# A two-block transformer's opening: small loads on the ACT queue, fewer warming products, two modulation rows moved past a phase border

## The reference, cut to what matters

```python
c_act = jax.nn.silu(c)                                    # c: (1, 1024)
mod = (c_act @ ada_w[layer] + ada_b[layer])[:, None, :]   # the modulation vectors
sh_a, sc_a, gt_a, sh_m, sc_m, gt_m = jnp.split(mod, 6, axis=-1)
h = rms_norm(x, attn_norm[layer]) * (1 + sc_a) + sh_a     # modulate
q, k, v = jnp.split(h @ w_in, 3, axis=-1)                 # diff_attention, head by head
```

## Time and profile before

| | us |
|---|---|
| median of three runs | 2323.18 |
| the three runs | 2322.82, 2323.18, 2329.31 |
| the profiled execution | 2325.73 |
| its span in the profile | 2324.0 |
| PE busy, share of the span | 2227.1 (96%) |
| DVE busy | 1222.9 (53%) |
| ACT busy | 518.9 (22%) |

### The profile page before, as it was taken

How to read it: one execution, slowest core, us unless ns; L and a number is a source line. 1 busy time by engine, 2 the same in 40 slices (tenths; PEclk the granted TensorE clock), 3 DMA queues, 4 the chain that set the end, 5 groups by cost and what they waited for, 6 DMA issues and landing times. The chain is left out here.

```text
span 2324.0 us, 26617 instructions
## 1 busy us (share of the span) xinstructions
PE 2227.1 (96%) x9804; PEld 1495.2 (64%) x9804; DVE 1222.9 (53%) x2805; ACT 518.9 (22%) x1187; POOL 41.4 (2%) x49
## 2 busy tenths in 40 slices
PE   8999999999999999999999999999999899999976
PEld 4444688888887555558888888854578444444332
DVE  5455666667766266676655767668565311111104
ACT  4333223230003244442323100112232000000001
POOL 0000000000000000000000000000000010000100
PEclk9999999999999999999999999999998999999998
DMA  9455123534433211114534435311032799999996
GB/s 361 170 199 199 73 73 150 213 145 181 181 145 118 73 55 55 56 45 153 209 146 184 178 149 204 155 72 73 1 145 96 290 427 426 426 427 424 426 427 249
DMA packets 46419, 452.07 MB, mean 195 GB/s; under 512 B 7560, under 2 KB 8840, under 8 KB 21456
## 3 DMA queue, kind: packets, MB, share of 16 engines
q1 hardware_dynamic: 39440, 436.04, 47.0%
q0 software_dynamic: 6240, 12.17, 1.4%
q10 hardware_dynamic: 608, 2.14, 0.2%
HBM read 443.36 MB, written 17.87 MB: 198 GB/s over the span
## 5 line engine op out<-in xcount | busy, mean ns | idle before, releaser
L1404 PE MATMUL ps<-big,ring 128*128 128x256 f32 x768 | 186.0, 379 | 0.6 <-PE ps L1319 0.6
L3282 PE MATMUL ps<-big 128*64 128x512 f32 (+1 forms) x416 | 171.6, 606 | 7.8 <-ACT big L3337 5.0
L1319 PE MATMUL ps<-hT,ring 128*128 128x256 f32 x768 | 178.2, 380 | 0.0
L1319 PEld LDWEIGHTS ps<-hT,ring 128*128 128x128 f32 x768 | 144.8, 190 | 23.1 <-ACT hT L452 4.0
L1404 PEld LDWEIGHTS ps<-big,ring 128*128 128x128 f32 x768 | 145.6, 190 | 21.0 <-issue 1.4
L584 PE MATMUL ps<-hT,ring 128*128 128x512 f32 x336 | 151.7, 600 | 0.0
L3282 PE MATMUL ps<-ring,big 128*64 128x512 f32 (+1 forms) x336 | 134.0, 594 | 11.4 <-ACT big L3337 6.6
L2333 PE MATMUL ps<-hT,ring 128*128 128x512 f32 x320 | 140.7, 594 | 2.7 <-DVE big L2715 1.7
L1216 DVE SCALAR_TENSOR_TENSOR ring<-ring,tmp 128x1024 f32<-128x1024 f32 x112 | 136.3, 1218 | 0.0
L1404 PE MATMUL ps<-oT 128*128 128x256 f32 x512 | 120.8, 379 | 2.1 <-DVE oT L1583 2.1
L1319 PE MATMUL ps<-oT 128*128 128x256 f32 x512 | 115.8, 379 | 0.0
(11 more groups left out here) (550 smaller groups left out, 3893.7 us busy)
## 6 DMA issues: line engine op xcount, KB each, us to landing
ring<-in_stream SPq DMA_DIRECT2D x98, 2048.0 KB, 8.8
big<-in_up SPq DMA_DIRECT2D x18, 2048.0 KB, 22.7
ring<-in_down SPq DMA_DIRECT2D x17, 2048.0 KB, 22.0
ring<-in_gate SPq DMA_DIRECT2D x15, 2048.0 KB, 22.9
big<-in_gate SPq DMA_DIRECT2D x10, 2048.0 KB, 20.4
big<-in_down SPq DMA_DIRECT2D x8, 2048.0 KB, 21.9
ring<-in_up SPq DMA_DIRECT2D x6, 2048.0 KB, 18.8
oT<-in_up SPq DMA_DIRECT2D x5, 2048.0 KB, 28.2
```

The source lines that it names most:

```text
L1319: ins = pe.matmul(place(i, name), a[:, k, :], b[:, k, :], start=(k == 0), stop=(k == 3))
L1404: ins = pe.matmul(m.ps[:, bank[name], q * H:(q + 1) * H], a[:, q * P:(q + 1) * P], b, start=(first and q == 0), stop=(final and q == 1))
L3282: ins = pe.matmul(out[a:z, :], left[:, k * P + a:k * P + z], bufs[j][:, k * width + c * 512:k * width + (c + 1) * 512], start=(k == 0), st ...
```

## The change

It moves three loads from SP's queue to ACT's, ahead of ACT's first wait; it takes four of the six warming products between the sums and the spreading of the norm out; and it moves rows 2 and 3 of chunk 0, with the release of its slot, from `phase_start` to `phase_diff`, behind the first tile of `unit_rows`. The waits on `first_done` are counted anew.

```diff
@@ phase_start, sync
-                sp.dma_start(m.vec[:, 0:VEC_FIRST], m.d_vec[:, 0:VEC_FIRST]).then_inc(small, 16)
-                sp.dma_start(con(m, "ident"), m.d_con[:, 0:P]).then_inc(consts, 16)
-                sp.dma_start(buckets(m.con), buckets(m.d_con)).then_inc(consts, 16)
                 sp.dma_start(m.xT[:], m.d_x.rearrange("(k p) t -> p k t", p=P)).then_inc(xin, 16)
@@ phase_start, scalar
+                act.dma_start(m.vec[:, 0:VEC_FIRST], m.d_vec[:, 0:VEC_FIRST]).then_inc(small, 16)
+                act.dma_start(con(m, "ident"), m.d_con[:, 0:P]).then_inc(consts, 16)
+                act.dma_start(buckets(m.con), buckets(m.d_con)).then_inc(consts, 16)
                 act.wait_ge(small, 16)
@@ phase_start, vector
                 dve.reciprocal(m.st[:, 0:NT], m.st[:, 0:NT]).then_inc(inverse, 1)
-                for j in range(2, 4):
-                    first_modulation(m, dve, 0, j, crow).then_inc(mod_done, 1)
-                dve.wait_ge(mod_done, 4)
-                dve.sem_inc(m.free[0], 1)
+                dve.wait_ge(mod_done, 2)
@@ phase_start, tensor
-                keep_busy(m, pe, 0, 6)
+                keep_busy(m, pe, 0, 2)
@@ phase_diff, scalar
-                    if k >= 2:
-                        act.wait_ge(first_done, 2 * k - 2)
+                    if k:
+                        act.wait_ge(first_done, 2 * k)
@@ phase_diff, vector, first_columns
-                    dve.wait_ge(m.full[n % RING], 16 * (n // RING + 1))
-                    for j in range(4):
-                        first_modulation(m, dve, c, j, crow).then_inc(first_done, 1)
-                    dve.wait_ge(first_done, 4 * c)
+                    if c:
+                        dve.wait_ge(m.full[n % RING], 16 * (n // RING + 1))
+                    for j in range(4 if c else 2):
+                        first_modulation(m, dve, c, j if c else 2 + j, crow).then_inc(first_done, 1)
+                    dve.wait_ge(first_done, 4 * c + 2)
                     dve.sem_inc(m.free[n % RING], 1)
@@ phase_diff, vector
-                for c, tiles in ((1, range(0, 3)), (2, range(3, 6)), (3, range(6, KT))):
+                for c, tiles in ((0, range(0, 1)), (1, range(1, 3)), (2, range(3, 6)), (3, range(6, KT))):
                     for k in tiles:
                         unit_rows(k)
                     first_columns(c)
```

## The result

The changed kernel took 2336.85 us in the median of six runs (2333.64 to 2339.97), the kernel before 2327.89 beside it: ratio 1.0046, interval 1.0032 to 1.006. A second comparison of the same two, twelve runs against 35, gave 1.0033 (1.0022 to 1.0043). That is 8 to 11 us slower, at or over the 0.3% (7 us) that can be told; 2325.9 had been forecast, within 2321.4 to 2329.2. One run of a later kernel, the moved rows alone, took 4002.93 us at a granted clock of 0.628 and is left out of its ratio.

What follows compares the result with a forecast made beforehand. DVE's and PE's lines were both taken to bind the opening, with PE busy behind it. Rows and warming +1.2 plus moved loads +1.5 gave +2.7 us on 2323.18: 2325.9, range 2321.4 to 2329.2.

Steps and rivals of the forecast that it cites:

- Moved loads: Opening, three small loads on ACT's queue: x's packets beside them delay the tables by 1.5 us, bounds -0.2 and +3.3.
- The vector starts level with x: Opening loads: reason for taking 1.5 us, nearer the lower end, instead of the 40 KB store's 3.3.
- rival C: Opening: x goes ahead of the tables; tables +3.3 to +4.8 us, sum +4.5 to +6.0, up to 2329.2; chance 0.21.
- The lower bound: Moved loads: -0.2 us, by three issues at the 0.35 of ACT's row instead of about 0.42.
- E: Opening: ACT loads its table first and issues the loads from 2.03, 1.3 us more, 2327.2; chance 0.03.
- Warming products and moved rows: Before the first head's projection: border 1.08 us earlier, DVE's line to tile 6 1.36 later, PE gets it 1.2 later.
- B: Opening: tables land as before or 0.2 sooner, PE's line decides, warming products give 1.7 us; 2321.4; chance 0.12.
- Handed on as it is: Behind the opening: PE is busy without pause, so any shift of the opening's end passes on unchanged.
- One sign of being wrong: Behind 60 us: the prediction is wrong if stretches there differ in length.
- D: First head's projection: TensorE's clock stays at half throughout, +19 us, 2342; chance 0.02.

Runs made afterwards that it cites:

- the delays of 2, 3, 5 and 9 fills: The kernel before with the opening's loads held back by 2, 3, 5 or 9 one-tile fills on DVE: ratios 1.0013, 1.0024, 1.0014, 1.0033.

## Why the prediction was wrong

**Moved loads: the step that failed.** "One x packet between each two: 18 x 0.084 = +1.5", taken between -0.2 and +3.3. It measured **+3.9**, beyond the upper bound I gave the term. "The vector starts level with x" was true of the vector, which came 1.1 late. The tables are issued 0.47 and 0.95 behind it, and by then x had the engines: that is rival C's place and mechanism, given 0.21, and its price for the tables (+3.3 to +4.8) held the measured one. That the head's end came to C's far +6.0 is luck: C had 4.8 for the tables there, and nothing for the sums below. The 5.7 us of the small transfer on ACT's queue was the nearest row, and I set it aside as a store behind a long backlog; x alone is backlog enough. The lower bound fell too, as ACT's issues took 0.43 to 0.45 each and not 0.35; and so did E, as ACT issued at 0.75.

The Trainium skill, page "DMA: Bandwidth & Descriptors", section "Issuing engines are not separate DMA queues", says that such transfers interleave on the same 16 engines; the two kernels with x and the small loads apart and swapped agree (2.3 and 6.6 us). Its "Queues, rings and completion order" has an engine drain a packet of typically 9 to 17 descriptors from one queue before it turns; the trace's 153 packets of x in 4 to 5 us (2 KB each, 9.6 for each engine), with none of ACT's queue, are in line with that. The order within one engine was not seen.

**Warming products and moved rows: right, in mechanism and size.** Without the moved loads the border came 1.18 earlier (1.08 forecast), tile 6 came 1.36 later (1.36), and the head's end 0.95 and 1.16 later (1.2). DVE's line, with 0.15 of slack, did take back more than the warming gave. B, by which PE's line decides, is refuted.

**The sums: not foreseen.** In the changed kernel's first profile 3.89 at the bias product becomes 3.58 at ACT's copy and 4.99 at ACT's root. In between lie the sums over partitions, 6.99 us instead of 5.58. Their rows, of the changed kernel, of before and of the loads alone:

```profile
16.89 6.99 PE L344 MATMUL ps<-ones,hT 128*128 128x1 f32 x32 [2.05 <-DVE hT L318]
```

```profile
13.31 5.58 PE L347 MATMUL ps<-ones,hT 128*128 128x1 f32 x32 [1.36 <-DVE hT L318]
```

```profile
17.17 4.96 PE L347 MATMUL ps<-ones,hT 128*128 128x1 f32 x32 [1.24 <-DVE hT L318]
```

One row of the changed kernel, 17 to 24 us, and two of before, 13.31 to 15 and 15 to 22 us, show the clock:

```profile
17.00:24.00 7.00, 7.00 (x33) 7.00 (x34) 4.37 (x7) 3.73 (x8) 0.00 (x0) 0.50 1.02 412
```

```profile
13.31:15.00 1.69, 1.69 (x15) 1.69 (x15) 1.12 (x2) 1.69 (x5) 0.00 (x0) 1.00 0.91 384
15.00:22.00 7.00, 7.00 (x34) 7.00 (x35) 5.68 (x11) 2.33 (x5) 0.00 (x0) 0.51 1.02 413
```

Before, the first 1.7 us of the sums ran at full clock, 2.4 GHz; after, nearly all of them at half. The late tables alone don't bring this: the kernel with the loads alone has the same program up to there and took 4.96, at a granted clock of 0.98 from 17 to 20 us. Why the clock fell where it did is open. So 3.9 - 0.3 + 1.4 - 1.1 + 2.5 - 0.4 = 6.0 at the head's end, where 2.7 was forecast: the tables missed by 2.4, the sums by 1.4, and the rest came out some 0.5 better than its 1.2.

**"Handed on as it is": not quite.** Behind the head's end 2.4 us more came in the first profile, and 8 to 11 us in time stand against 6.0. Three stretches of before, and of the changed kernel's first profile cut at the same instructions:

```profile
60.42:250.10 189.68, 189.68 (x631) 93.01 (x630) 94.37 (x253) 56.72 (x147) 0.00 (x0) 1.00 0.49 180
250.10:350.12 100.02, 96.20 (x473) 81.06 (x472) 69.23 (x137) 27.61 (x58) 0.00 (x0) 0.95 0.18 64
700.14:760.34 60.20, 59.63 (x238) 40.72 (x236) 35.14 (x68) 17.53 (x28) 2.13 (x4) 0.97 0.27 111
```

```profile
66.41:256.09 189.68, 189.68 (x631) 93.01 (x630) 94.44 (x253) 56.73 (x147) 0.00 (x0) 1.00 0.49 180
256.09:357.29 101.20, 97.40 (x474) 81.11 (x473) 69.30 (x137) 27.58 (x58) 0.00 (x0) 0.95 0.17 63
707.31:769.08 61.77, 61.20 (x238) 42.29 (x236) 35.13 (x68) 17.54 (x28) 2.13 (x4) 0.94 0.27 107
```

To 250 us the 5.99 is handed on whole. It grows by 1.2 and 1.6 in two stretches in which the granted clock falls, and PE is busy longer there for the same instructions; elsewhere it changes by 0.4 at most. One sign of being wrong, stretches behind 60 us of another length, did come. D had the clock as the danger, but in the first projection, where DVE's line hides it.

The recorded clocks say how much of the time this is. In the runs of the kernel before, one us of clock time lost (one minus the mean granted clock, times the span) goes with about 0.7 us of time. With that taken off the difference of the means, an estimate, the changed kernel (second comparison) is 6.3 us up, where its head's end is 6.1 late; the loads alone 4.0 (3.4), the rows alone 2.2 (2.9), two warming products alone 0.8 down (0.5 earlier), all but the loads 2.2 and 1.8 up (1.0 and 1.2), x held back 1.6 (2.8), the delays of 2, 3, 5 and 9 fills 2.2, 3.2, 4.3 and 7.0 (3.2, 2.2, 3.1 and 5.6). Only x on ACT's queue falls out, 5.1 (8.5). So the time follows the head's end within about 1.4 us, and most of what lies beyond is clock. Whether the edits themselves make the later stages lose more clock is open: all but the loads had 0.9796 and 0.9795 against 0.9813 beside it both times, the loads alone 0.982.

**The basis.** I counted from 2323.18, the median of three runs. The comparisons' medians of the same kernel lie at 2325.87 to 2329.58. Of the miss of 10.95 us, 4.7 is this (2327.89 - 2323.18), the other 6.3 is 8.96 measured beside it (by the medians) against 2.7 forecast. The range took its width from the terms alone and none from the 6.5 us over which the runs shown were spread.

No version tried beats the kernel before by more than the rounds can tell. Two warming products alone end the first head 0.56 us earlier in their one profile, which is the best seen there.

## What to carry to other kernels

Small transfers that the first step waits for went better ahead of a large one than beside it: issuing them on another queue took 1.2 us of issue time off SP, and put the tables 3.9 us later. Before work is moved from an engine's idle time into its chain, look for the slack at the point where that chain and the bound engine meet: 0.15 us of slack decided here against 2.4 us of moved rows. Where a program's time spreads over several us from run to run, the forecast's basis and its range must carry that spread; and where the granted clock explains the spread, differences are best taken at equal clock.

## What the hardware showed unexpectedly

Of three small loads issued 0.5 us apart beside a 2 MB transfer, the first landed 1.1 us late and the others 4.2 (6.7 for 2.5) with x on SP's queue; with x on ACT's it was 0.5 and 4.1 (6.6).

TensorE's clock fell in the midst of its sums: in before it was busy without pause from 13.31, and still the granted clock went from 1.00 to 0.5 at about 15. It was back at 1.00 from 22 us on, during the spread.

The spread from run to run is mostly the clock: over the 35 runs of the kernel before beside the first four experiments, 2321.31 to 2334.32 us, the time goes with the clock time lost with a correlation of 0.91.
